# Two transformer blocks in float32: the sums for twenty units of layer-two modulation weights move from the feed-forward stages to the first perceptron of the second block

## The reference

```python
for i in range(DEPTH):                      # DEPTH = 2
    mod_l = (c_act @ ada_w[i] + ada_b[i])[:, None, :]
    mod_c = cc_act @ ada_w[i] + ada_b[i]
    sh_a, sc_a, g_a, sh_m, sc_m, g_m = jnp.split(mod_l, N_MOD, axis=-1)
    ...
    x = x + g_a * y_l
    x = x + g_m * sq_relu_mlp(modulate(rms_norm_2(x, norm_mlp_g[i]), sh_m, sc_m), mlp_w1[i], mlp_w2[i])
    if need_ctx_out: ...                    # the same for the context, layer 0 alone
```

## Time and profile before

| | |
|---|---|
| median of 3 runs | 2474.45 us (2474.43 to 2484.86) |
| the profiled execution | 2472.36 us, its span 2470.2 us |
| TensorE busy | 2410.9 us, 98% of the span |
| VectorE, ScalarE, GpSimd busy | 1614.7, 1198.3, 322.8 us |
| HBM read | 394.72 MB, 161 GB/s over the span |
| granted TensorE clock | 0.992 of full speed |

### The profile page before, as it was taken

How to read it: one execution, slowest core, us unless ns; L and a number is a source line. 1 busy time by engine, 2 the same in 40 slices (tenths; PEclk the granted TensorE clock), 3 DMA queues, 4 the chain that set the end, 5 groups by cost and what they waited for, 6 DMA issues and landing times.

```text
span 2470.2 us, 40328 instructions
## 1 busy us (share of the span) xinstructions
PE 2410.9 (98%) x17021; PEld 2213.1 (90%) x17021; DVE 1614.7 (65%) x2448; ACT 1198.3 (49%) x1987; POOL 322.8 (13%) x362
## 2 busy tenths in 40 slices
PE   8999989999999998999999999999999999999998
PEld 7999879999999998899999767888888888889998
DVE  5687666788888876768775875542443664566753
ACT  6444566544444456655554553531332544445643
POOL 1321000332022110031442000100000100001000
PEclk9999999999999999999999999999999999999999
DMA  7767644576777766357776120233223333334552
GB/s 237 235 219 202 187 147 124 182 241 221 257 239 244 233 162 201 107 148 262 264 271 194 52 82 18 88 100 102 89 99 103 131 102 120 102 120 154 171 190 101
DMA packets 374088, 401.51 MB, mean 163 GB/s; under 512 B 44695, under 2 KB 346035, under 8 KB 373652
## 3 DMA queue, kind: packets, MB, share of 16 engines
q1 hardware_dynamic: 371160, 391.19, 49.6%
q10 hardware_dynamic: 2748, 7.76, 0.9%
HBM read 394.72 MB, written 4.19 MB: 161 GB/s over the span
## 4 chain that ended last, share of the span: by engine, by line
PE 74%; DVE 15%; ACT 4%; DMA 3%; issue 2%; POOL 1%; SPq 1%; ACTq 0%; DVEq 0%; POOLq 0%
PE bank L686 22%; PE bank L688 22%; PE bank L687 22%; DVE rounded L2466 7%; PE bank L694 3%; DVE plain L2451 3%; ACT rounded L1672 2%; DMA plain<-in_w_in 2%; PE bank L699 2%; DMA plain<-in_ffn_w_down 1%; POOL plain L3547 1%; PE bank L1113 1%; DVE plain L2598 1%; PE bank L1143 1%; SPq L3669 0%
## 5 line engine op out<-in xcount | busy, mean ns | idle before, releaser
L686 PE MATMUL bank<-rounded 128*128 128x256 f32 (+2 forms) x3480 | 1082.7, 311 | 8.7 <-DVE rounded L2466 4.1
L687 PE MATMUL bank<-rounded 128*128 128x256 f32 (+2 forms) x3480 | 1066.7, 307 | 0.0
L688 PE MATMUL bank<-rounded 128*128 128x256 f32 (+2 forms) x3480 | 1066.5, 306 | 0.0
L2466 DVE TENSOR_TENSOR rounded<-plain,rounded 128x1024 fp32r<-128x1024 f32 (+1 forms) x630 | 742.4, 1225 | 411.4 <-ACT rounded L1672 411.2
L1672 ACT ACTIVATE rounded<-plain 128x1024 fp32r<-128x1024 f32 (+1 forms) x630 | 616.6, 1032 | 392.1 <-PE bank L688 272.2
L686 PEld LDWEIGHTS bank<-rounded 128*128 128x128 f32 x3480 | 666.9, 192 | 59.2 <-issue 10.1
L688 PEld LDWEIGHTS bank<-rounded 128*128 128x128 f32 x3480 | 666.8, 192 | 28.9
L687 PEld LDWEIGHTS bank<-rounded 128*128 128x128 f32 x3480 | 667.4, 192 | 28.1
L686 PE MATMUL bank<-rounded,rounded 128*128 128x256 f32 (+2 forms) x1472 | 449.9, 306 | 9.2 <-DVE plain L2671 3.2
L687 PE MATMUL bank<-rounded,rounded 128*128 128x256 f32 (+2 forms) x1472 | 446.6, 303 | 0.0
L688 PE MATMUL bank<-rounded,rounded 128*128 128x256 f32 (+2 forms) x1472 | 446.4, 303 | 0.0
(11 more groups left out here) (311 smaller groups left out, 1890.1 us busy)
## 6 DMA issues: line engine op xcount, KB each, us to landing
plain<-in_mlp_w SPq DMA_DIRECT2D x64, 1024.0 KB, 5.2
plain<-in_ada_w SPq DMA_DIRECT2D x48, 1024.0 KB, 5.7
plain<-in_ffn_w_gate SPq DMA_DIRECT2D x44, 1024.0 KB, 5.3
plain<-in_ffn_w_up SPq DMA_DIRECT2D x44, 1024.0 KB, 6.1
plain<-in_ffn_w_down SPq DMA_DIRECT2D x32, 1024.0 KB, 5.4
plain<-in_w_in SPq DMA_DIRECT2D x32, 1024.0 KB, 5.4
plain<-in_od_w_in SPq DMA_DIRECT2D x32, 1024.0 KB, 5.3
plain<-in_ffn_w_down SPq DMA_DIRECT2D x16, 768.0 KB, 5.1
```

The source lines that it names most:

```text
L686: pe.matmul(dst, a[0], b[0], start=first and i == 0, stop=False)
L687: pe.matmul(dst, a[0], b[1], start=False, stop=False)
L688: ins = pe.matmul(dst, a[1], b[0], start=False, stop=last and i == n - 1)
L2466: dve.tensor_tensor(low, raw, top, SUB).then_inc(*done(("lo", m, half)))
```

## The change

Of the 48 units the first 28 (chunks 0 to 6) stay in the feed-forward stages, 4, 8, 8 and 8 of them, four steps apart for the most part; the last 20 (chunks 7 to 11, of the second layer) stand in p0, behind w1 units 2 to 5, behind all eight w2 units of its first half, and behind all eight w1 units of its second half. The sums of these lie in the norm's scratch (`modacc`, 2 x 1024 words from BASE: the scratch's rstd, both squares and one temporary). VectorE's first sum of chunk 7 waits for the end of p0's first product, which reads that scratch, and ScalarE's squares at p0's end wait for the turns of chunks 10 and 11.

```diff
--- before.py
+++ after.py
@@ -92,10 +92,9 @@
 
 CHUNKS = ([(0, ch, (0, 1)) for ch in range(6)] + [(1, ch, (0, 1)) for ch in range(2)] + [(1, ch, (0,)) for ch in range(2, 6)])
 
-ADA = {"a0": [7, 11, 15, 19, 22, 24, 26, 28], "b0": [1, 4, 6, 9, 12, 14, 17, 19, 23, 26, 28, 31],
-       "a1": [1, 4, 6, 9, 12, 14, 17, 19, 23, 25, 27, 30],
-       "b1": [1, 3, 5, 7, 9, 11, 13, 15, 17, 19, 21, 23, 25, 27, 29, 31]}
-ADA_AT = {(s, step): u for u, (s, step) in enumerate((s, step) for s in ("a0", "b0", "a1", "b1") for step in ADA[s])}
+ADA = {"a0": [13, 17, 22, 26], "b0": [1, 5, 9, 13, 17, 21, 25, 29], "a1": [1, 5, 9, 13, 17, 21, 25, 29],
+       "b1": [2, 6, 10, 14, 18, 21, 25, 29], "p0": [2, 3, 4, 5, *range(8, 24)]}
+ADA_AT = {(s, step): u for u, (s, step) in enumerate((s, step) for s in ("a0", "b0", "a1", "b1", "p0") for step in ADA[s])}
 
 
 def turns():
@@ -105,7 +104,7 @@
         if u % 4 == 3:
             for v in CHUNKS[u // 4][2]:
                 at = step + v
-                out[(s, at) if at < 33 else ({"b0": "a1"}[s], at - 33)] = (u // 4, v)
+                out[s, at] = (u // 4, v)
     return out
 
 
@@ -474,6 +473,7 @@
 
     def lay_mlp(self):
         self.mlp = []
+        self.modacc = [self.words(self.BASE + 1024 * i, 1024) for i in range(2)]
         for n, part in ((512, 16), (256, 32)):
             b = Box()
             self.top = self.PHASE2
@@ -549,7 +549,9 @@
 
     def acc(self, n, v):
 
-        return self.ffn.acc[2 * (n % 2) + v if len(CHUNKS[n][2]) == 2 else 2 + n % 2]
+        if n < 7:
+            return self.ffn.acc[2 * (n % 2) + v]
+        return self.modacc[v if n == 7 else n % 2]
 
     def plan_ffn(self, s, name, l):
         wg, wu, wd = (self.t[f"{name}_w_{n}"][l] for n in ("gate", "up", "down"))
@@ -624,9 +626,11 @@
         for half in range(b.seqs):
             for blk in range(b.part // 2):
                 self.square((s, "w1", half, blk), self.t["mlp_w1_2"][l], 0, 8, (half * b.part + blk * 2) * 128, 256)
+                self.plan_ada(s, 16 * half + blk)
             for blk in range(4):
                 for k0 in range(0, b.part, 8):
                     self.square((s, "w2", half, blk, k0), self.t["mlp_w2_2"][l], half * b.part + k0, 8, blk * 256, 256)
+                    self.plan_ada(s, 16 * half + 8 + 2 * blk + k0 // 8)
 
     def plan_odd(self):
         w, wo = self.t["od_w_in_2"][0], self.t["od_w_out_2"][0]
@@ -1478,6 +1482,7 @@
                         keys = [("unit", m)] if j else []
                         product(bs[j][:, 0:n], [(part(m, k, j * 128), hx(k, 0, n)) for k in range(8)]).then_inc(
                             *done((s, "w1", half, 2 * blk + j), *keys))
+                fill(s, 16 * half + blk)
             for blk in range(4):
                 if (l, half, blk) == (0, 1, 3):
                     bs = {(q, j): bank(s, "w2", 1, 6 + j, q) for q in (1, 0) for j in range(2)}
@@ -1510,6 +1515,7 @@
                                           k == 0, k == b_.part - 1)
                         keys = [("unit", m)] if j else []
                         ins.then_inc(*done((s, "w2", half, 2 * blk + j, k0), *keys))
+                    fill(s, 16 * half + 8 + 2 * blk + k0 // 8)
                     if l and (blk, k0) == (2, 0):
                         for tile in range(2):
                             outward(bank("out", tile, 0), tile, 0, 4)
@@ -2292,18 +2298,22 @@
                         act.wait_ge(*x)
                     act.activation(b_.hr[:, c, :], r, ACT.Copy, scale=1.0).then_inc(*done((s, "hidhi", half, c)))
                 hi(U[s, "w1", half, blk] + 3)
+                fill(s, 16 * half + blk)
             for blk in range(4):
                 for k0 in range(0, b_.part, 8):
                     last = half == b_.seqs - 1
                     if last and k0 == b_.part - 8 and not (l == 0 and blk == 3):
                         for j in range(2):
                             o = 2 * blk + j
+                            for x in new(at("ada", 10, 0, 1), at("ada", 11, 0, 1)):
+                                act.wait_ge(*x)
                             square(s, o, at(s, "x", half, o), 0, n, M.two.sq)
                             if l and o < 7:
                                 act.activation(M.F[:, o, :], X[:, o, 0:256], ACT.Copy, scale=col("final_g_2", o)).then_inc(
                                     *done(("out", "F", o)))
                     if not (last and blk == 3 and k0 == b_.part - 8):
                         hi(U[s, "w2", half, blk, k0] + 3)
+                        fill(s, 16 * half + 8 + 2 * blk + k0 // 8)
         if l == 0:
             turn("o", s, lambda c, q: M.MODS[1][:, c, q:q + 1])
         here("end", s, "act")
@@ -2442,7 +2452,7 @@
                 keys = [("fma", n, v, k)] + ([("unit", m)] if i and v == vecs[-1] else [])
                 if k == 0:
                     last = [(a, w) for a in range(n) for w in CHUNKS[a][2] if M.acc(a, w) is acc]
-                    for s in new(at("raw", m), at("ada", *last[-1], 1) if last else None):
+                    for s in new(at("raw", m), at("ada", *last[-1], 1) if last else None, at("p0", "w1", 0, 0) if n == 7 else None):
                         dve.wait_ge(*s)
                     dve.tensor_scalar(acc, raw[:, i, :], M.cc[:, k, v:v + 1], None, MUL).then_inc(*done(*keys))
                 else:
```

## The result

The changed kernel took 2487.09 us (median of 11 runs, 2477.38 to 2493.02) against 2474.45 for the kernel before (11 runs beside it, 2472.38 to 2484.86); the ratio over all runs is 1.0042, 95% interval 1.0027 to 1.0056 (the two medians alone give 1.0051). The forecast was 2484.0 (a ratio of 1.0039), with a range of 2464 to 2492. In a second comparison (further down) the ratio was 1.0022 (1.0009 to 1.0036). So the change costs a few tenths of a per cent. The profiled execution's span went from 2470.2 to 2480.4 us.

What follows compares the result with a forecast made beforehand. TensorE was taken to set the time, so only its idle time counts: -12.5 + 9.4 + 7.3 + 1.0 + 0.3 = +5.5 us, plus 4 of slow clock, net +9.5, giving a median of 2484.0 us, range 2464 to 2492.

Steps and rivals of the forecast that it cites:

- What goes: TensorE waits behind splits in a0, b0, a1, and a0's 3.2 us bank wait with 2.6 us slow clock, vanish: -12.5 us.
- The four waits of 2.35 us: Down parts of a0, b0, a1, b1: new TensorE waits for a PSUM bank freed by a residual, +9.4 us in all.
- the old wait: a0's down part in the kernel before: TensorE waits 3.21 us for a PSUM bank that VectorE's residual frees.
- the first rival: The bank waits at the takes of d5, d7 and gu8b don't bind, so the kernel is faster: 2463.2 us; chance 0.15.
- The wait in b1: b1 at block 8: TensorE waits 4.7 us for gu7a's bank, plus 2.6 us of slow clock, +7.3 us.
- The clock behind the short waits: After the four waits of 2.35 us: half pull the clock down at 2.0 us each, +4 us, range 0 to 10.4.
- two rows: Profile rows: after 2.55 us idle the clock was 0.77 (1.5 us lost); after 2.12 us it stayed 1.00.
- 13, 14 in b0 and a1: Turn steps 13, 14: no bank wait, but the split of g9 late by about 0.5 us in each, +1.0 us.
- p0: p0 steps 2 to 4: two-vector sums use up VectorE's slack by step 4, +0.3 us (0 to 3).
- the third rival's p0 part: p0's steps 3 to 5 run some 2 us late; with all four clock falls, 2492.4 us; the rival's chance 0.2.
- The stages: Signs by stage: b1 longer by about 9 us, a0 shorter by 3 to 5 us.
- The sum: Whole kernel: -12.5 + 9.4 + 7.3 + 1.0 + 0.3 = +5.5 us, with +4 for the clock net +9.5 us.

Runs made afterwards that it cites:

- second comparison: The changed kernel, unaltered, measured again beside the kernel with all turns moved and the residual ahead of the split: 2483.79 us, ratio 1.0022 to the kernel before.
- The run without the respacing: Changed kernel's move of twenty units to p0, but the first 28 units and their turns on the steps of the kernel before: 2474.7 us, ratio 0.9992.
- the run that removed this one wait alone, one turn of the kernel before moved: Kernel before with only a0's turn of modulations at steps 28, 29 moved to 30, 31: 2477.01 us, ratio 0.9995.
- the run with the residual first: Changed kernel with VectorE's residual ahead of the weight split in the down parts, turns and units left alone: 2469.7 us, ratio 0.9964.
- the one with b1's turn moved: Changed kernel with only the turn of modulations at b1's steps 14, 15 moved to 15, 16: 2475.12 us, ratio 0.9989.
- all five turns moved: Changed kernel with five turns of modulations one step later (a0 27, 28; b0, a1, b1 30, 31; b1 15, 16): 2464.3 us, ratio 0.9942.
- shifted parity: Changed kernel with five turns one step later, and also b0's and a1's turns of steps 13, 14 moved to 14, 15: 2476.61 us, ratio 0.9993.

## Why the prediction was right

The mechanism was right in its places, its releasers and nearly its sizes; that the total came so close is in part luck, as the points on the clock and on the sum show.

- **What goes.** The waits behind the splits went in a0, b0 and a1, and a0's 3.2 us with its slow clock: -12.5 us of the profile as worked out. The run without the respacing keeps 5.2 of the 6.3 us behind splits, so most of them went with the spacing, as the step had it. For the 5.8 us in a0 the waits are shown and the time isn't: the run that removed this one wait alone measured 1.8 us.
- **The four waits of 2.35 us** came as 2.31, 2.32, 2.32 and 2.38 us, each at the named take, each released by the residual. The arithmetic (the old wait less eight transposes) was all there was to it, because the chain begins with TensorE's own last matmul and doesn't depend on load. That also is why the first rival fell. Its argument that VectorE's load drops in all four stages was wrong for b1 (154.9 us before, 158.9 after).
- **The wait in b1** was put at 4.7 and was 4.89 us, with 2.6 us of slow clock as forecast. Each term came as booked: both halves of the split 3.45 us (1209.26 to 1212.71), reductions and addition 1.4, the two products 0.75. The price of the clock is less firm than one profile makes it look: behind a wait of 4.89 us at the same place 1.5 us were lost in the run with the residual first (26 matmuls in 4.6 us).
- **The clock behind the short waits.** Half of four at 2.0 us, +4, was the choice between two rows. Of the twelve such waits in three profiles (the changed kernel twice, and the one with b1's turn moved) six were followed by the lower level, three, two and one of four; each fall cost some 1.5 us. In the compared profile it was three, 4.8 us together. Over the twelve the half was right and the price of 2.0 us high; in the compared profile the two errors partly cancel. The lower of the two rows was weaker than it looked: the same wait of 2.12 us, after which the clock stayed at 1.00, was followed by long slow stretches in four other profiles (last section).
- **13, 14 in b0 and a1** were booked at +0.5 us each and cost nothing: no TensorE wait stands there in b0 or a1.
- **p0** was booked at +0.3 and cost nothing. The timeline of VectorE in the changed p0:

```profile
1617.11 4.87 DVE L2461 SCALAR_TENSOR_TENSOR plain<-plain 128x1024 f32<-128x1024 f32 x4
1621.89 2.35 DVE L2476 TENSOR_TENSOR rounded<-plain,rounded 128x1024 fp32r<-128x1024 f32 x2
```

  The split is done at 1624.2, and TensorE, which ends w1's fourth unit at 1614.3 and the fifth at 1625.2, wants it at 1625.2: 1.0 us of room where the prediction had 0.2 at this step, so the third rival's p0 part had no place.
- **The stages.** b1 was to be 9 us longer and a0 3 to 5 us shorter; they came out at 11.9 and 5.9. For b1 the forecast's own terms make 9.65 us (7.3 and 2.35) before any slow clock behind the short wait, which took 1.6 more. For a0 the sign left out the sixteen transposes that moved away, 1.7 us.
- **The sum.** Added in the profile: 14.2 us of idle time, 2.6 + 4.8 of slow clock; gone: 12.5; net 9.1 of the 10.2 us that the span grew. A fall of the clock in the even mixer (below), which the forecast didn't have, added 1.7 us. Against that, b0 and a1 came out about 1 us each better than waits, transposes and slow clock add up to; why is open. So 1.3 us were booked for waits that never came, and slow clock that wasn't booked took their place. The mean granted clock went from 0.992 to 0.988. By the medians the change cost 12.6 us in the first comparison and 7.0 in the second; the forecast of 9.5 lies between.

## What to carry to other kernels

When buffers are dealt in a fixed rotation, a cheap extra user between two takes matters by how many buffers it takes, not by how long it holds them: seven takes behind decides who waits, and the wait is the whole chain of the engine that frees the buffer, including work that it only has ahead of it in program order. Before moving such a user, write out the takes around its new place. Relief of a busy engine paid here only where some wait ended behind that engine: VectorE lost 24 to 27 us of work in three stages, and what could be gained by it were waits of some 6 us in all, most of which went only when the work that stayed was spaced out.

## What the runs showed of the hardware that was not expected

- The same idle time doesn't always have the same sequel. In the even mixer TensorE idles 1.70 us in both kernels, at 1430.70 before and 1433.95 after; before the granted clock stayed at 1.00, after it was 0.68 over the next 5.3 us (first row before, second after):

```profile
1430.70:1434.00 3.30, 3.09 (x20) 2.17 (x21) 3.16 (x8) 3.30 (x6) 0.00 (x0) 1.00 0.02 5
...
1433.90:1439.20 5.30, 5.04 (x21) 3.53 (x22) 4.97 (x13) 4.67 (x12) 0.00 (x0) 0.68 0.00 0
```

  and the waits of 2.3 us were followed by a fall in six of twelve cases at the same places of the program. A larger case is the wait of 2.12 us in the even mixer. Here are the same 14 us of the changed kernel in its first profile and in its second; at half clock 7 of the 14 us are lost:

```profile
1476.00:1490.00 14.00, 14.00 (x43) 6.43 (x39) 9.36 (x14) 6.60 (x11) 0.00 (x0) 1.00 0.23 75
...
1476.00:1490.00 14.00, 14.00 (x28) 6.16 (x24) 9.55 (x14) 3.42 (x7) 0.00 (x0) 0.51 0.24 75
```

  The profiles of three other versions (all five turns moved, one turn of the kernel before moved, shifted parity) have such a stretch there too, 14 us at 0.51 to 0.53. No version changes this stage, so one profile beside another can differ by 7 us without any cause in the edit, and only many runs of each kernel can be compared. Among the eleven runs of the changed kernel the fastest has the highest mean clock (0.991) and the slowest the lowest (0.986).
- Most waits repeat from profile to profile: the same wait for a bank to within 0.01 us (2.31 or 2.32, 2.38 or 2.39, 4.89 us), and behind the splits of b0's and a1's blocks 1.07, 0.58, 0.93 and 0.59 us to within 0.03 us in three versions. What differs between the kernel before and the same with one turn of a0 moved are two waits in the down parts: b0's of 1.3 us is new, a1's has 2.5 us instead of 1.5. Followed back from 841 us, the chain of a1's wait passes a residual and comes to an upper half for which ScalarE waited until a down weight had landed. First in the kernel before, then in the other, whose TensorE was 0.8 us earlier there:

```profile
824.52 2.01 ACT L1672 ACTIVATE rounded<-plain 128x1024 fp32r<-128x1024 f32 x2 [8.72 <-DMA plain<-in_ffn_w_down]
...
825.07 2.01 ACT L1675 ACTIVATE rounded<-plain 128x1024 fp32r<-128x1024 f32 x2 [10.06 <-DMA plain<-in_ffn_w_down]
```

  So the longest wait behind a split has a load in its chain and not VectorE's sums alone, and a stage with fewer loads may shorten it by that way too. No run tells the two apart, and for the one in b0 the cause is open.
